# Dilated attention: the keys' square sums as two fp32r products of high and low parts, the low parts made on GpSimd

## The reference, cut to what matters

```python
B_GROUPS = 3
B_HEADS = 16
B_HEAD_DIM = D_MODEL // B_HEADS
...
def _rms(x, gain):
    xf = x.astype(jnp.float32)
    y = xf * lax.rsqrt(jnp.mean(xf * xf, axis=-1, keepdims=True) + EPS)
    return (y * gain.astype(jnp.float32)).astype(x.dtype)
...
def _shared_kv(x, kv_norm, w_kv, k_gain):
    bsz, seq, _ = x.shape
    kv = (_rms(x, kv_norm) @ w_kv).reshape(bsz, seq, 2, B_GROUPS, B_HEADS, B_HEAD_DIM)
    k = _rms(kv[:, :, 0], k_gain[:, None, :])
    v = kv[:, :, 1]
```

## Time and profile before

| | |
|---|---|
| median of 3 runs | 2555.39 us (2554.95 to 2556.24) |
| profiled execution, its own time | 2556.5 us |
| its span, first to last instruction | 2554.7 us |
| TensorE busy | 2489.3 us (97%) |
| VectorE busy | 1744.9 us (68%) |
| ScalarE busy | 1316.9 us (52%) |
| GpSimd busy | 79.0 us (3%) |
| mean granted clock of TensorE | 0.995 |

### The profile page before, as it was taken

One profiled execution on the slowest core, in us unless ns is written; L12 is line 12 of the kernel. 1 busy time (PEld: TensorE's weight loads), 2 busy tenths in 40 slices (PEclk: granted clock), 3 DMA queues, 4 the chain that ended last, 5 costly groups with the idle time before them and its releaser, 6 DMA issues.

```text
span 2554.7 us, 60487 instructions
## 1 busy us (share of the span) xinstructions
PE 2489.3 (97%) x23329; PEld 2423.8 (95%) x23329; DVE 1744.9 (68%) x2871; ACT 1316.9 (52%) x1997; POOL 79.0 (3%) x122
## 2 busy tenths in 40 slices
PE   8998998999999999999999999899999999999999
PEld 8997977989999999989999999899999999999999
DVE  6757677567766757767766767967667666666774
ACT  5534444455545546555545547455455455555552
POOL 0000442000000000000000000000000000000000
PEclk9999999999999999999999999999999999999999
DMA  6663301435655656445655655246656665553664
GB/s 203 218 211 125 100 12 44 149 126 181 208 185 188 212 202 185 153 136 182 207 181 188 211 176 190 75 126 201 203 173 201 200 188 153 157 157 111 195 210 136
DMA packets 119840, 425.14 MB, mean 166 GB/s; under 512 B 16673, under 2 KB 24564, under 8 KB 119412
## 3 DMA queue, kind: packets, MB, share of 16 engines
q1 hardware_dynamic: 111616, 411.65, 49.7%
q10 hardware_dynamic: 8052, 11.04, 2.3%
HBM read 421.51 MB, written 1.12 MB: 165 GB/s over the span
## 4 chain that ended last, share of the span: by engine, by line
PE 87%; DVE 5%; ACT 3%; issue 2%; POOL 1%; SPq 0%; DMA 0%; ACTq 0%; DVEq 0%; POOLq 0%
PE bank L492 20%; PE bank L487 20%; PE bank L491 20%; PE bank L410 5%; PE bank L415 4%; PE bank L414 4%; ACT hi L348 1%; PE bank L2410 1%; DVE lo L356 1%; PE bank L468 1%; PE bank L470 1%; PE bank L469 1%; PE bank L1812 1%; PE bank L1785 1%; PE bank L1797 1%
## 5 line engine op out<-in xcount | busy, mean ns | idle before, releaser
L356 DVE TENSOR_TENSOR lo<-raw,hi 128x1024 fp32r<-128x1024 f32 (+1 forms) x728 | 935.3, 1293 | 381.0 <-ACT hi L348 379.2
L348 ACT ACTIVATE hi<-raw 128x1024 fp32r<-128x1024 f32 (+1 forms) x728 | 782.2, 1106 | 292.9 <-PE bank L415 168.1
L487 PE MATMUL bank<-Hh,hi 128*128 128x256 f32 x3024 | 836.3, 277 | 3.1 <-DVE lo L356 2.0
L492 PE MATMUL bank<-Hh,lo 128*128 128x256 f32 x3024 | 837.4, 277 | 0.0
L491 PE MATMUL bank<-Hl,hi 128*128 128x256 f32 x3004 | 830.1, 276 | 0.0
L487 PEld LDWEIGHTS bank<-Hh,hi 128*128 128x128 f32 x3024 | 567.9, 188 | 4.3 <-DVE lo L356 4.0
L492 PEld LDWEIGHTS bank<-Hh,lo 128*128 128x128 f32 x3024 | 568.1, 188 | 0.0
L491 PEld LDWEIGHTS bank<-Hl,hi 128*128 128x128 f32 x3004 | 564.3, 188 | 0.0
L487 PE MATMUL bank<-Ah,hi 128*128 128x256 f32 x1408 | 389.7, 277 | 1.9 <-DVE lo L356 1.9
L492 PE MATMUL bank<-Ah,lo 128*128 128x256 f32 x1408 | 390.1, 277 | 0.0
L491 PE MATMUL bank<-Al,hi 128*128 128x256 f32 x1400 | 387.2, 277 | 0.0
(11 more groups left out here) (445 smaller groups left out, 4042.3 us busy)
## 6 DMA issues: line engine op xcount, KB each, us to landing
raw<-in_w SPq DMA_DIRECT2D x600, 512.0 KB, 3.7
raw<-in_w SPq DMA_DIRECT2D x128, 704.0 KB, 4.9
dB<-dil_bias ACTq DMA_DIRECT2D x16, 384.0 KB, 10.4
X<-in_x SPq DMA_DIRECT2D x2, 512.0 KB, 5.9
mem_x<-in_mem ACTq DMA_DIRECT2D x2, 512.0 KB, 4.4
gWS<-in_ws ACTq DMA_DIRECT2D x1, 1024.0 KB
gBS<-in_bs ACTq DMA_DIRECT2D x1, 1024.0 KB
out_x<-X SPq DMA_DIRECT2D x4, 256.0 KB, 2.6
```

Of the source, the lines that this page charges most:

```text
L348: act.activation(k.hi[:, q, :w], k.raw[:, q, :w], ACT.Copy).then_inc(k.hi_ready, 1)
L356: dve.tensor_tensor(k.lo[:, q, :w], k.raw[:, q, :w], k.hi[:, q, :w].bitcast(F32), ALU.subtract).then_inc(k.lo_ready, 1)
L487: pe.matmul(out, wh, xh, start=first, stop=False)
L492: mm = pe.matmul(out, wl, xh, start=False, stop=last)
```

## The change

The 768-column square becomes three squares of 256 columns that write fp32r (`KSQh`); the first stands one step earlier than the one square did. GpSimd makes each group's low part: it multiplies the keys by themselves in float32 (`KK`, one buffer for all groups) and subtracts the high part (`KSQl`). TensorE multiplies each with `HO`, a copy of the head ones in fp32r that GpSimd makes once, and adds both in the same bank. TensorE now waits by group, for the square and for the low part, in place of once for all squares.

```diff
-        self.KSQ = k.at("dKSQ", a + 9 * KB, [P, GROUPS, T])
+        self.KSQh = k.at("dKSQh", a + 9 * KB, [P, GROUPS, T], F32R)
+        self.KSQl = k.at("dKSQl", a + 39 * KB, [P, GROUPS, T], F32R)
+        self.KK = k.at("dKK", a + 42 * KB, [P, T])
+        self.HO = k.at("dHO", a + 43 * KB, [P, P], F32R)
...
     def pe_key_sums(self, pe, c):
 
         k = self.k
-        k.act_done.wait(pe, f"d.ksq{c}")
         if c:
             k.act_done.wait(pe, f"d.pt{c - 1}.1")
         for g in range(GROUPS):
             out = k.bank[5][:, g * T:(g + 1) * T] if g < 2 else k.bank[6][:, :T]
-            ins = pe.matmul(out, k.head_ones, self.KSQ[:, g, :], start=True, stop=True)
+            k.act_done.wait(pe, f"d.ksq{c}.{g}")
+            k.pool_done.wait(pe, f"d.ksl{c}.{g}")
+            pe.matmul(out, self.HO[:], self.KSQh[:, g, :], start=True, stop=False)
+            ins = pe.matmul(out, self.HO[:], self.KSQl[:, g, :], start=False, stop=True)
         k.pe_done.done(ins, f"d.ks{c}")
...
                 if i == (4 if c else 6):
                     self.act_query_scales(act, c)
+                if i == (4 if c else 1):
+                    self.act_key_squares(act, c, 0)
                 if i == (5 if c else 2):
-                    k.dve_done.wait(act, f"d.kraw{c}")
-                    d(act.activation(self.KSQ[:], self.K[c % 2][:], ACT.Square), f"d.ksq{c}")
+                    self.act_key_squares(act, c, 1)
+                    self.act_key_squares(act, c, 2)
...
+    def act_key_squares(self, act, c, g):
+
+        k = self.k
+        act.wait_ge(k.banks_freed, RING + self.slab(c, "k", g) + 1)
+        k.act_done.done(act.activation(self.KSQh[:, g, :], self.K[c % 2][:, g, :], ACT.Square), f"d.ksq{c}.{g}")
+
+    def pool(self, pool):
+
+        k = self.k
+        for c in range(NC):
+            for g in range(GROUPS):
+                pool.wait_ge(k.banks_freed, RING + self.slab(c, "k", g) + 1)
+                if c == g == 0:
+                    k.pool_done.done(pool.tensor_copy(self.HO[:], k.head_ones), "d.ho")
+                if c and g == 0:
+                    k.pe_done.wait(pool, f"d.ks{c - 1}")
+                x = self.K[c % 2][:, g, :]
+                if c or g:
+                    k.pool_done.wait(pool, f"d.ksl{c}.{g - 1}" if g else f"d.ksl{c - 1}.{GROUPS - 1}")
+                k.pool_done.done(pool.tensor_tensor(self.KK[:], x, x, ALU.mult), f"d.kk{c}.{g}")
+                k.act_done.wait(pool, f"d.ksq{c}.{g}")
+                k.pool_done.wait(pool, f"d.kk{c}.{g}")
+                k.pool_done.done(pool.tensor_tensor(self.KSQl[:, g, :], self.KK[:], self.KSQh[:, g, :].bitcast(F32), ALU.subtract),
+                                 f"d.ksl{c}.{g}")
...
         @block.gpsimd
         def _(pool):
             for b in body:
-                if isinstance(b, Rwkv7):
+                if isinstance(b, (Rwkv7, Dilated)):
                     b.pool(pool)
```

## The result

The changed kernel takes 2565.5 us in the median of 20 runs (2560.6 to 2576.77), the kernel before in the same sets of runs 2554.39 (2550.03 to 2561.76). The ratio is 1.0047, with a 95% interval of 1.0036 to 1.0058: by the ratio 12.0 us slower, between 9 and 15; the two medians lie 11.1 us apart. The profiled execution has a span of 2563.1 us, 8.4 more than before.

The account below looks back on a forecast made before the run. TensorE, busy 97% of the span, was taken to bound the kernel. Waits in chunks 1 to 7 (+3.5), chunk 0 (+3.35) and a clock fall (+1.5) gave +8.35 us on 2555.39: 2563.7 us, range 2557 to 2571.

Parts of the forecast that it names:

- The saving if nobody is late: TensorE's key sums, chunks 1 to 7: 0.80 us to the next work in place of 1.39, seven chunks -4.1 us.
- ScalarE: Dilated attention: three squares of 256 columns fit between existing work, and the probabilities behind them start no later.
- GpSimd's durations: Per chunk three multiply and subtract pairs: 0.73 us per instruction, 0.08 between them, 0.06 for a semaphore between engines.
- The collision: Chunk 1: GpSimd's subtract 1 waits for VectorE's low part, ending 0.59 us behind it; TensorE's next work +0.50 us.
- the seven chunks: Chunks 1 to 7 of the dilated attention, alike, each +0.50 us as TensorE waits for GpSimd: +3.5 us.
- Chunk 0's wait: Chunk 0's key sums: GpSimd and VectorE block each other, TensorE idles some 2.2 and 2.3 us: +3.35 us.
- The clock: Behind chunk 0's stall TensorE's granted clock falls once to 0.50 for 3.40 us: +1.5 us, bounds 0 and 3.
- The sum: Whole kernel: 3.5 + 3.35 + 1.5 = +8.35 us on 2555.39, giving 2563.7 us, 0.33% more.
- No blocking: Rival: GpSimd and VectorE pass each other in the dilated attention; net -0.1 us, 2555.3 us. Chance 0.10.
- a slow fp32r store: Rival: GpSimd's fp32r store or restart is slow; 0.1 us more each costs 2.4 us, 1.0 gives 2570. Chance 0.13.
- a clock that holds: Rival: blocking as forecast, but the clock does not fall behind chunk 0; +6.85 us, 2562.2 us. Chance 0.14.
- The sums that never wait: Rival: TensorE's key sums never wait for GpSimd; -4.1 us and 1.2 more in chunk 0, 2550.1 us. Chance 0.03.

Follow-up runs that it names:

- e5: Changed kernel with three float32 buffers, multiplies before subtracts, and VectorE's low part behind GpSimd's last subtract; ratio to the kernel before 0.9979.
- e7: Changed kernel, but GpSimd makes no low parts and the second product takes the high part again; ratio to the kernel before 0.9968.
- e3: Changed kernel, but VectorE's low part of the weights waits for GpSimd's last subtract, so the two can't run together; ratio to the kernel before 1.0001.
- a0: The changed kernel run again without edit; ratio to the kernel before 1.0025.
- a1: The changed kernel run once more without edit, in a later set of runs; ratio to the kernel before 1.0041.
- e1: Changed kernel, but chunk 0 computes its key sums as before the change; ratio to the kernel before 1.0015.
- e2: Changed kernel, but in chunk 0 TensorE runs 15 products into an unused bank before group 1 and 15 before group 2; ratio to the kernel before 1.0031.
- e2b: Repeat of e2, the changed kernel with products filling chunk 0's two waits; ratio to the kernel before 1.0027.
- e9: Chunk 0 alone as changed, chunks 1 to 7 as in the kernel before; ratio to the kernel before 1.0026.
- e4: Changed kernel, but each group has its own float32 buffer and GpSimd makes all three multiplies before the first subtract; ratio to the kernel before 1.0005.
- e8: Chunks 1 to 7 with the edits of e5, chunk 0 with float32 sums as before the change; ratio to the kernel before 0.9979.
- e6: Kernel before, with GpSimd doing the same multiplies and subtracts beside it for nobody; ratio to the kernel before 0.9998.

## Why the prediction was right, point by point

**The saving if nobody is late, 0.59 us.** Right for the sums themselves (0.81 us in e5 against the 0.80 worked out), but not all: chunks 1 to 7 gain 0.75 each in e5 and e7. The other 0.17 lies in the two slabs behind the sums, below.

**ScalarE.** Hidden, as said. The first square of chunk 1 ends at 2113.29 and the high part behind it begins at 2113.90, its usual place.

**GpSimd's durations.** The multiply takes 0.61 and not 0.73; the subtract that writes fp32r 0.73, as taken; the copy of the head ones 0.29, hidden. From one of its instructions to the next it is 0.14 to 0.15 and not 0.08 (2116.81 to 2116.96, 2117.57 to 2117.71), and from the end of the subtract (2118.44) to the product 0.15 and not 0.06. By luck the errors nearly cancel: behind the collision they leave 0.10 us.

**The collision.** This step carried the forecast and held in its detail: 0.59 us behind the end of the low part, the subtract of group 1 at 1.47, the others of chunk 1 at 0.73. e3 shows the cause. The Trainium skill ("SBUF — State Buffer", the section on the two separate sides) has it that whichever of the two starts first holds the shared ports for its whole instruction; the chain of chunk 0, with 1.67, 1.52, 1.40 and 1.41 us in turn, agrees, and VectorE's evacuation from PSUM in the middle of it took its usual 0.41. The last pair was to start 1.46 us behind the first product; it starts 1.56 behind. The next work was to be 0.50 late and is 0.57 late. Against that stand the quicker slabs, so the seven chunks cost 2.7 us in place of the 3.5 of the sum (2.9 to 3.4 in a0, a1, e1, e2 and e2b).

**Chunk 0's wait.** +3.35 forecast, +3.22 in e2 and e2b, where the clock holds. In the changed kernel's first trace TensorE stands idle 1.95 us twice, 3.9 in all, where over 4 was named. Both blockings of GpSimd and both of VectorE came as listed.

**The clock.** The fall came in every trace in which chunk 0 is as changed and nothing fills its waits: for one stretch in a0, a1 and e9, for two in the first trace. One was taken at 1.5 us and costs 1.3 to 1.6; two cost 2.8. e2 and e2b show that without the idle time it does not come. But the forecast had it from one of two rows that were alike, and idle time alone does not settle it here either. The first line is chunk 0 of e3, after which the clock held; the other two are chunk 0 of e4 and the stretch behind it, where 0.64 is the mean of full clock and of 0.50:

```profile
2068.75:2072.15 3.40, 1.02 (x5) 0.70 (x5) 0.19 (x1) 1.62 (x4) 2.67 (x4) 1.00 0.52 77
...
2064.25:2067.65 3.40, 1.07 (x6) 0.59 (x4) 2.90 (x3) 2.02 (x5) 2.98 (x3) 1.00 0.47 67
2067.65:2071.05 3.40, 3.10 (x17) 3.13 (x18) 0.00 (x0) 1.89 (x3) 0.16 (x1) 0.64 0.85 116
```

TensorE was as little busy in both, 1.02 and 1.07 of 3.40 us. What decides between them is not shown, so it was in part luck that the forecast's one fall came, and came once in three traces of four.

**The sum.** +8.35 forecast, +7.8, +7.9 and +8.7 in the stage by three traces. In the first of these traces two errors cancel: the seven chunks cost 0.8 less than the sum has, the clock 1.3 more. The time itself is nearer than the increase, since the 2555.39 that the forecast started from, a median of 3 runs, lies 1.0 us above the 2554.39 of the 20. The timed runs gave +12.0, then +6.4 and +10.5. What the first set has above the stage's loss, some 3 us, is not explained. The arrival at the stage's norm scatters by 8 us over the traces of all kernels (2058.20 in e2, 2066.36 in e1), before TensorE has come to anything that is changed, and the difference between the sets may be no more than that; this was not tested.

**The rivals.** No blocking is refuted by e3 and the trace; a clock that holds by four traces; a slow fp32r store by 0.73, while its restart is 0.07 us slower than taken. The sums that never wait came true only once the order was changed, in e5 and e8. The forecast thought six GpSimd instructions had to be hidden behind the last square; with three buffers the multiplies wait for no square, and only subtracts are left there. The 2.5 us given there between the last square and the use is nearer 1.9 by the forecast's own times (2110.10 to 2111.97).

## What to carry to other kernels

When work moves to GpSimd, place its instructions in time beside VectorE's: when both had one with two SBUF inputs here, the one that started second waited until the other had ended, and the price was what stood behind it on the path: nothing in e6, some 8 us with the clock's fall in the changed kernel. A gain on TensorE comes out only if the helper's last result is there first; here a wait on an engine with 3.5 us to spare turned a loss of some 8 us into 0.4. The first round of a stage deserves its own account: it was built in another order, and it held two thirds of the loss.

## What the runs showed of the hardware beyond that

The slabs behind the sums run at two paces. In chunk 1 of the kernel before, eight products of line 415 in the slab behind line 1812 start from 2114.69 to 2117.16, 0.353 us for three products; in the changed kernel the eight of the same slab, behind line 1817:

```profile
2120.79 0.28 PE L415 MATMUL bank<-Kh,lo 128*128 128x256 f32 x1
...
2123.19 0.28 PE L415 MATMUL bank<-Kh,lo 128*128 128x256 f32 x1
```

That is 0.343 us for three, 0.07 us less for a slab. The faster pace stands in both slabs behind the sums in the first trace of the changed kernel, e4, e5, e7 and e8, and the slower one in both in e6 and e9, where the sums of chunks 1 to 7 are float32 as before. In e3, with fp32r sums, the first slab has the slower pace and the second the faster. In the repeated traces of the changed kernel the first slab differs from chunk to chunk, slower in three of seven in a0 and in six of seven in a1, and a chunk with the slower one is 0.12 us longer (36.11 in place of 35.99 from sums to sums). That makes most of the difference between 252.56 and 253.19 us in the table. The kernel before has both paces too: the slab in front of the sums runs at 0.341 us for three. So the form of the sums alone doesn't set the pace; what does is open. It is worth 0.17 us a chunk, over a fifth of what e5 gains.
